# State-space stage: two tensor products moved from GpSimd to VectorE, behind the addition to the state

## The reference, cut to what matters

```python
decay_to_end = jnp.exp(a_cs[..., -1:] - a_cs)
states = jnp.einsum('bclgn,bcgel,bclgep->bcgepn', bc, decay_to_end, xs)
chunk_decay = jnp.exp(a_cs[..., -1])
def step(h, inp):
    st, dec = inp
    return h * dec[..., None, None] + st, h
```

## Time and profile before

| what | before |
|---|---|
| median of 3 runs | 2407.63 us (2406.78 to 2408.15) |
| the profiled execution | 2409.64 us, of which 2407.9 us is the span from the first to the last instruction |
| busy share of the span | PE 95%, DVE 73%, ACT 35%, POOL 9% |
| state-space stage, first `diff` to the first matmul of the output projection | 1347.17 to 1477.88 us, 130.71 us |
| in this stage | PE 93.38, DVE 88.38, ACT 55.76, POOL 47.17 us busy; 16 POOL instructions |

### The profile page before, as it was taken

How to read it: one execution, slowest core, us unless ns; L and a number is a source line. 1 busy time by engine, 2 the same in 40 slices (tenths; PEclk the granted TensorE clock), 3 DMA queues, 4 the chain that set the end, 5 groups by cost and what they waited for, 6 DMA issues and landing times. The chain is left out here.

```text
span 2407.9 us, 29647 instructions
## 1 busy us (share of the span) xinstructions
PE 2284.5 (95%) x10470; PEld 1863.1 (77%) x10470; DVE 1762.8 (73%) x2675; ACT 847.5 (35%) x1300; POOL 224.3 (9%) x188
## 2 busy tenths in 40 slices
PE   7999999999999999999999787998999999999996
PEld 6888888888878777778778565887788888888885
DVE  8877777777588878877573477777787777777766
ACT  6322222222344655556223443212432222222222
POOL 0000000000001333323000245400000000000000
PEclk9999999999999999999999888999899999999998
DMA  4111111112331010101112322312411111111122
GB/s 152 53 53 52 52 52 52 52 52 78 105 115 45 18 36 18 36 18 36 44 44 96 124 79 87 97 46 86 140 48 53 52 52 52 52 52 52 48 96 105
DMA packets 52326, 155.62 MB, mean 65 GB/s; under 512 B 5904, under 2 KB 7952, under 8 KB 50064
## 3 DMA queue, kind: packets, MB, share of 16 engines
q1 hardware_dynamic: 52240, 154.51, 19.4%
HBM read 133.18 MB, written 21.30 MB: 64 GB/s over the span
## 5 line engine op out<-in xcount | busy, mean ns | idle before, releaser
L1009 DVE TENSOR_TENSOR acc<-psum,acc 128x512 f32<-128x512 f32 x288 | 197.9, 691 | 160.7 <-PE psum L595 158.0
L593 PE MATMUL psum<-act_hi,tile_hi 128*128 128x512 f32 x704 | 276.9, 393 | 11.9 <-DVE acc L617 7.1
L594 PE MATMUL psum<-act_lo,tile_hi 128*128 128x512 f32 x704 | 275.7, 392 | 0.0
L595 PE MATMUL psum<-act_hi,tile_lo 128*128 128x512 f32 x704 | 275.6, 391 | 0.0
L708 ACT CAST t_hi<-t_raw 128x512 fp32r<-128x512 f32 x144 | 89.8, 624 | 308.3 <-DVE t_raw L869 295.0
L593 PEld LDWEIGHTS psum<-act_hi,tile_hi 128*128 128x128 f32 x704 | 133.4, 189 | 41.9 <-DVE acc L617 9.5
L595 PEld LDWEIGHTS psum<-act_hi,tile_lo 128*128 128x128 f32 x704 | 133.3, 189 | 28.0
L594 PEld LDWEIGHTS psum<-act_lo,tile_hi 128*128 128x128 f32 x704 | 133.5, 190 | 27.5
L1853 DVE TENSOR_TENSOR probs_t_lo<-psum,probs_t_hi 128x512 fp32r<-128x512 f32 x144 | 96.8, 686 | 55.1 <-ACT probs_t_hi L1779 55.1
L730 ACT ACTIVATE sum<-sum 128x512 f32<-128x512 f32 x72 | 45.7, 635 | 245.8 <-DVE sum L963 151.2
L454 PE MATMUL psum<-norm_hi,plain_hi 128*128 128x512 f32 x288 | 112.0, 389 | 0.0
(11 more groups left out here) (373 smaller groups left out, 5741.2 us busy)
## 6 DMA issues: line engine op xcount, KB each, us to landing
tile_lo_raw<-in_d SPq DMA_DIRECT2D x40, 512.0 KB, 4.3
gate_raw<-in_gu SPq DMA_DIRECT2D x36, 512.0 KB, 4.0
up_raw<-in_gu SPq DMA_DIRECT2D x72, 256.0 KB, 3.6
raw_tile<-in_w_xz SPq DMA_DIRECT2D x19, 512.0 KB, 3.6
gate_up_lo_raw<-in_gu SPq DMA_DIRECT2D x8, 1024.0 KB, 5.1
cum_rows<-cum_scratch SPq DMA_DIRECT2D x8, 1024.0 KB, 4.8
raw_tile<-in_w_out SPq DMA_DIRECT2D x16, 512.0 KB, 3.6
raw_tile<-in_w_att SPq DMA_DIRECT2D x11, 512.0 KB, 3.5
```

The lines of the kernel that those rows point to most:

```text
L593: pe.matmul(o, w_h[:, s, d, :], a_h[:, s, x], start=(s == 0), stop=False)
L594: pe.matmul(o, w_h[:, s, d, :], a_l[:, s, x], start=False, stop=False)
L595: mm = pe.matmul(o, w_l[:, s, d, :], a_h[:, s, x], start=False, stop=(s == 1))
L1009: v.tensor_tensor(x, banks(4 + d % 4), x, ALU.add).then_inc(sem(p + "_acc"), 1)
```

## The change

Both products, with the same operands, buffers and semaphores, are issued by VectorE. For chunk 0 they stand between `x_and_cb(0)` and `mix(0)`; for chunk c+1 they stand behind `state(c)` and ahead of `diff(c+2)`. `ssd_pool` goes, and GpSimd has nothing to do in this stage.

```diff
+            def decayed(c):
+                wait(v, "sd_st", c)
+                v.tensor_tensor(hp[:], st[:], row_of("chd", c), ALU.mult).then_inc(sem("sd_hp"), 1)
+
+            def to_end(c):
+                v.wait_ge(sem("sd_xt"), c + 1)
+                wait(v, "sd_st_mm", c)
+                v.tensor_tensor(xw[:], xt[:], row_of("wend", c), ALU.mult).then_inc(sem("sd_xw"), 1)
+
             v.wait_ge(sem("xz_mm"), 2 * (XBC_T + Z_T))
             diff(0)
             v.memset(st[:], 0.0).then_inc(sem("sd_zero"), 1)
             x_and_cb(0)
+            v.wait_ge(sem("sp_act"), 6)
+            v.wait_ge(sem("sp_step"), 15)
+            to_end(0)
+            v.wait_ge(sem("sd_zero"), 1)
+            decayed(0)
             mix(0)
             diff(1)
             for c in range(CH):
@@
                 output(c)
                 state(c)
+                if c + 1 < CH:
+                    to_end(c + 1)
+                    decayed(c + 1)
                 if c + 2 < CH:
                     diff(c + 2)
@@
-        def ssd_pool(g):
-            ...
-            g.wait_ge(sem("sd_zero"), 1)
-            g.wait_ge(sem("sp_act"), 6)
-            g.wait_ge(sem("sp_step"), 15)
-            for c in range(CH):
-                to_end(c)
-                decayed(c)
@@
             att_pool(g)
-            ssd_pool(g)
             gate_pool(g)
```

## The result

| | before | after |
|---|---|---|
| median | 2408.26 us (6 runs, 2406.78 to 2410.83) | 2416.78 us (6 runs, 2413.96 to 2418.63) |
| ratio after to before | | 1.0031 (95% interval 1.0020 to 1.0042) |
| profiled execution, its span | 2409.64, 2407.9 us | 2413.96, 2412.2 us |
| stage, first `diff` to first matmul of the output projection | 130.71 us | 140.48 us |
| `diff(0)` to the first `act_lo` behind the scan | 128.25 us | 138.02 us |

The kernel became slower, by 8.5 us between the medians and by 7.5 us (4.8 to 10.1) by the ratio. The stage grew by 9.77 us; 2417.5 us and a stage of 140.6 us had been forecast.

The account below looks back on a forecast made before the run. A VectorE-ScalarE loop through diff, Relu, Exp and token copy was taken to bound the scan; 13.7 − 0.85 − 1.2 − 1.7, about +9.9 us on 2407.63, gave 2417.5 us (+0.41%), range 2412.5 to 2422.5.

Parts of the forecast that it names:

- The loop: Scan: diff, Relu, Exp, token copy, x_dt, cb, mix, output, state, next diff set the 13.30 us period.
- 13.7 for the pair: Scan, six turns: to_end and decayed ahead of diff cost 2.28 us each turn, +13.7 us.
- −1.18 for `mix(1)`: Chunk 1: the mix pair, stretched beside a to_end on GpSimd, falls from 3.54 to 2.36 us.
- rival A: Scan: VectorE's 3.6 us of idle gaps swallow the pair, only 3.75 us of relief is left: 2403.9 us; 5%.
- The head: Chunk 0: the pair ahead of mix(0) adds 2.28 us but mix(0) is no longer stretched: −0.85 us.
- Contention: Chunks 1 and 7: mix pairs stretched beside GpSimd's to_end return to 2.36 us, −1.18 and −1.70 us.
- Rival B: Scan: the freed port returns 30.4 us for 18.2 spent, −12 us, 2395.5 us; 3%.
- 13 of 16: Scan: count of GpSimd products that the kernel before already keeps off VectorE's critical path, said to speak against the change.
- The last turn: Behind state(6): no diff follows and off(7) waits for TensorE, so the pair costs nil.
- Nothing behind the scan can absorb it: After the scan: the output projection starts only after the last state with TensorE nearly full, so the +9.9 us stays.
- Rival C: Scan, tail and output projection: TensorE's lower clock or added waits lengthen the loop, +14 to +18 us, 2421.5 to 2425.5; 12%.

Follow-up runs that it names:

- the pair behind `diff`: The changed kernel with diff(c+2) issued first in each turn and the two products behind it: 2405.71 us, ratio 0.9986 to the kernel before.
- the pair twice: The changed kernel with both products issued a second time right behind the first, in the six turns where diff follows: 2427.17 us, ratio 1.0082 to the kernel before.
- the tokens early: The kernel before, with ScalarE's token copy for chunk c+2 ahead of that chunk's Relu and Exp; both products stay on GpSimd: 2395.71 us, ratio 0.9945.
- the kernel with the small products: The kernel before with both GpSimd products cut to one head of 16, the rest zeroed ahead of the scan: 2401.26 us, ratio 0.9969.
- the fastest kernel: Against before: token copy ahead of Relu and Exp, x_dt and cb ahead of off, VectorE's weight-split half moved behind the next turn's mix: 2387.76 us, ratio 0.9914.

## Why the prediction was right

**The loop.** Named from the earlier trace rows and shown: six turns from `x_dt(1)` to `x_dt(7)` took 85.60 us before and 98.01 after, +12.41. The prediction's terms are 13.7 for the pair and −1.18 for `mix(1)`; the pair measured 2.27 us a turn, 13.6 in sum. The two runs that carry it are the pair behind `diff` (2.27 us a turn gone at equal load, rival A's gap filled, but only from there) and the pair twice (another 13.6). Rival A, 2403.9 us, described the time of another kernel: it is near what the pair behind `diff` gives (2405.71). In the two turns with a weight split the chain isn't quite the one that the prediction names: behind the Exp stand both halves of the split and `off`, and the token copy is beside it. The pair is paid there all the same (17.87 against 15.61), as it stands ahead of `diff`.

**The head.** From `x_dt(0)` to `x_dt(1)`: 14.13 before, 13.31 after, −0.82; forecast −0.85.

**Contention.** All eight pairs of `mix` read 2.35 or 2.36 us after. From `x_dt(7)` to the first matmul of the output projection: 22.54 before, 20.72 after, −1.82; forecast −1.7. Sum −0.82 + 12.41 − 1.82 = +9.77, forecast +9.9. Rival B failed by its size: with GpSimd's products cut to one head of 16 the stage gave back 6.3 us, not 30. (The prediction's "13 of 16" products off VectorE's path should read 12: rival B itself lists four that aren't.)

**The last turn.** Forecast at nil, and so it is. The pair ends ahead of `off(7)`, which still waits for TensorE:

```profile
1472.59 1.21 DVE L2190 TENSOR_TENSOR state<-psum,state_decayed 128x1024 f32<-128x1024 f32 x1
1473.72 1.22 DVE L2199 TENSOR_TENSOR x_to_end<-x_tokens,wend 128x1024 f32<-128x1024 f32 x1
1474.86 1.22 DVE L2194 TENSOR_TENSOR state_decayed<-state,chd 128x1024 f32<-128x1024 f32 x1
1477.56 1.23 DVE L2178 TENSOR_TENSOR y_off<-psum,eac 128x1024 f32<-128x1024 f32 x1 [1.48 <-PE psum L2119]
```

**What fell short: "Nothing behind the scan can absorb it".** The profiled execution was 4.3 us longer, not 9.8. Ahead of the scan it was 0.6 later than before. Behind it the lead shrinks: +10.4 us at the first matmul of the output projection, +8.6 at its last, +9.0 at the first matmul of FFN 2 (1690.80, 1699.81) and +5.2 at the last of L541 there (1755.4, 1760.6). The work is the same; the windows from the first to the last of these L541 differ in TensorE's granted clock. Before, after, and after again, one fence each:

```profile
1690.80:1755.20 64.40, 64.40 (x320) 54.41 (x321) 49.07 (x53) 32.07 (x35) 0.00 (x0) 0.91 0.34 115
```
```profile
1699.81:1760.40 60.59, 60.59 (x321) 51.48 (x322) 49.05 (x53) 32.01 (x35) 0.00 (x0) 0.98 0.35 123
```
```profile
1699.56:1764.00 64.44, 64.44 (x320) 54.43 (x321) 49.08 (x53) 32.01 (x35) 0.00 (x0) 0.91 0.33 115
```

A mean of 0.91 against 0.98, with equal matmuls: 3.8 us. Another 1.4 us are gained between the first matmul of the output projection and that of FFN 2 (212.92 and 211.55 us, clock 0.94 and 0.95), and 0.9 behind this stretch. In the second profile of the changed kernel none of this is there: the lead is +8.7 us at the first matmul of the output projection and at the end alike, and that execution took 2418.40 us, 8.8 above the profiled one of before.

The pair-twice kernel, 3 us short of its expectation, was profiled in an execution of 2425.45 us, and its trace has the short stretch too (its four runs reach from 2424.19 to 2432.89, so the median alone says little):

```profile
1711.30:1771.90 60.60, 60.60 (x321) 51.47 (x322) 49.02 (x53) 32.00 (x35) 0.00 (x0) 0.98 0.35 122
```

These two are the only ones: in the other ten profiles (before, the changed kernel again, and the other variants) this stretch is at a clock of 0.91 or 0.92. The 13 runs of the changed kernel lie in two groups, 5 from 2412.28 to 2414.30 and 8 from 2416.49 to 2418.63 us; those of before lie together (2406.78 to 2411.30). The mean granted clock of the whole execution fits, but for one run: 0.977 or 0.978 in the short group, 0.974 to 0.976 in seven of the long one, and 0.978 in the eighth (2416.49). That every run splits for the same reason isn't shown, nor why the changed kernel meets the short stretch in some runs.

So the stage grew as forecast in every profile, and the whole time didn't. The medians of the two groups, 2417.5 and 2414.0 us, are some 9.2 and 5.7 above before, and the term that was missing is one of about −3.5 us in 5 runs of 13. That the median came out within 0.8 us of the 2417.5 forecast is in part luck: most runs fell into the longer group, and the median of before had gone up by 0.6. Rival C had the clock as a cost; it came as a gain.

**The port.** The Trainium skill ("SBUF — State Buffer", "Who interferes with whom") says that a VectorE instruction with two inputs in SBUF and a GpSimd instruction that reads SBUF exclude each other for a whole instruction and that issue order decides. The runs agree in every collision (3.99, 3.55, 2.92 us), and the kernel with only `to_end` moved adds what the order is when VectorE's instructions follow each other without a gap: GpSimd, which had asked during the first, came before the second.

## What to carry to other kernels

An engine that idles 3.7 us in a turn can still not take 2.3 us of work for free: what counts is whether the new instructions stand ahead of or behind the one that another engine is waiting for. Find in the timelines the step at which each link starts within 0.1 us of the one before, and put added work behind the last link that leaves the engine. And before moving work to relieve a loop, look whether a link is in it only by queue order, as the token copy was here: taking that one out made the stage 12.4 us shorter (8.9 in the turns, the rest in the last chunk), with nothing moved between engines. A turn in which the link wasn't on the chain, here the two with a weight split, gave nothing.

## What the runs showed of the hardware

- Moving one of two products cost more than moving both: stage +10.7 us against +9.8. A GpSimd instruction that is released while VectorE works takes the port between two back-to-back VectorE instructions, and the second took 3.99 instead of 2.28 us, six times of six.
- A collision at the port costs by place, not by count: `mix` was stretched in two of seven later chunks at a period of 13.3 us, in three at 14.5, in none at 10.7 to 11.0 with the tokens early, but for the first of them in the kernel that has only that change (3.58 us).
- TensorE's granted clock differed from turn to turn at one and the same period. In plain turns of 13.3 us it was 0.67 to 0.87, but 1.00 in one turn of 13.29 us of the kernel with the small products. With the tokens early it was 0.65 in the turn of 12.37 us and 1.00 in the two of 10.7, and in the fastest kernel 1.00 in all five turns from `x_dt(2)` on. At 1.00 TensorE was busy 9.6 us in a turn instead of 11.3. A bound for TensorE's chain that is read from slow windows is too high for windows at the higher level; that a shorter loop brings the clock up is not shown.
